# Sparse attention of a decoder trunk: branch order changed, compressed branch cut into 16 cells, window scores in row halves

## The reference, cut to what matters

```python
o_c = softmax(q @ ck.T * scale + bias, causal) @ cv      # 63 compressed keys per group
imp = sum over the group's heads of p_c @ ov             # importance of the 16 blocks of 64 keys
idx = top_k(forced or imp, 8)                            # 8 selected blocks per query
o_s = softmax over the keys of the selected blocks
o_w = softmax over the last 512 keys (sliding window)
o   = gate[0] * o_c + gate[1] * o_s + gate[2] * o_w
```

## Time and profile before

| | us |
|---|---|
| median of 3 runs | 2625.72 (2622.18 to 2634.36) |
| profiled execution | 2626.59 |
| its span | 2624.8 |

### The profile page before, as it was taken

How to read it: one execution, slowest core, us unless ns; L and a number is a source line. 1 busy time by engine, 2 the same in 40 slices (tenths; PEclk the granted TensorE clock), 3 DMA queues, 4 the chain that set the end, 5 groups by cost and what they waited for, 6 DMA issues and landing times. The chain is left out here.

```text
span 2624.8 us, 37850 instructions
## 1 busy us (share of the span) xinstructions
PE 2527.2 (96%) x14000; PEld 2049.3 (78%) x14000; DVE 1785.7 (68%) x2826; ACT 1124.4 (43%) x2184; POOL 1174.9 (45%) x889
## 2 busy tenths in 40 slices
PE   8999889999999999999988999999999999999999
PEld 5777667888887878887876688888788888777887
DVE  6554755477678999853059567666546767899993
ACT  4626544253334434323135566666524333433431
POOL 5362666234445444442236444444633444444441
PEclk8999999999999999999987899999999999999999
DMA  4010003224343544230342423222132334354531
GB/s 168 33 49 33 1 1 117 93 81 161 140 169 134 188 170 146 83 127 32 102 118 65 129 59 100 54 54 54 56 125 79 146 135 170 109 209 149 175 125 65
DMA packets 90973, 275.76 MB, mean 105 GB/s; under 512 B 9879, under 2 KB 38935, under 8 KB 76135
## 3 DMA queue, kind: packets, MB, share of 16 engines
q1 hardware_dynamic: 87240, 255.18, 28.4%
q10 hardware_dynamic: 3552, 18.18, 1.8%
HBM read 197.50 MB, written 73.86 MB: 103 GB/s over the span
## 5 line engine op out<-in xcount | busy, mean ns | idle before, releaser
L1582 PE MATMUL ps<-U_hi,RH 128*128 128x512 f32 x912 | 356.7, 391 | 12.5 <-DVE H L905 4.8
L1586 PE MATMUL ps<-U_lo,RH 128*128 128x512 f32 x912 | 355.7, 390 | 0.0
L1587 PE MATMUL ps<-U_hi,RL 128*128 128x512 f32 x912 | 355.6, 390 | 0.0
L1040 POOL TENSOR_TENSOR RL<-RAW,RH 128x512 fp32r<-128x512 f32 x112 | 156.2, 1395 | 395.2 <-ACT RH L744 395.2
L744 ACT ACTIVATE RH<-RAW 128x512 fp32r<-128x512 f32 x280 | 175.5, 628 | 292.8 <-PE ps L1587 285.4
L1533 POOL TENSOR_SCALAR PX<-PX,rinv,GATE 128x640 f32<-128x640 f32 (+7 forms) x256 | 197.8, 783 | 209.0 <-DVE rinv L3303 209.0
L1582 PE MATMUL ps<-U_hi,W_hi 128*128 128x512 f32 (+2 forms) x656 | 261.9, 399 | 13.3 <-DVE U_lo L2805 10.7
L1582 PE MATMUL ps<-SH,RH 128*128 128x512 f32 x656 | 256.8, 392 | 8.2 <-DVE H L905 4.1
L1586 PE MATMUL ps<-U_lo,W_hi 128*128 128x512 f32 (+2 forms) x656 | 258.2, 394 | 0.0
L1587 PE MATMUL ps<-U_hi,W_lo 128*128 128x512 f32 (+2 forms) x656 | 258.1, 393 | 0.0
L1586 PE MATMUL ps<-SL,RH 128*128 128x512 f32 x656 | 255.9, 390 | 0.0
(11 more groups left out here) (390 smaller groups left out, 6005.9 us busy)
## 6 DMA issues: line engine op xcount, KB each, us to landing
W_raw<-in_pieces SPq DMA_DIRECT2D x30, 1024.0 KB, 5.1
RAW<-in_pieces SPq DMA_DIRECT2D x28, 1024.0 KB, 4.9
RAW<-in_pieces SPq DMA_DIRECT2D x56, 512.0 KB, 7.7
hid_d<-HOA SPq DMA_DIRECT2D x24, 1024.0 KB, 3.9
hid_d<-HOB SPq DMA_DIRECT2D x24, 768.0 KB, 5.4
RHA<-hid_d SPq DMA_DIRECT2D x12, 1024.0 KB, 5.1
RHB<-hid_d SPq DMA_DIRECT2D x12, 768.0 KB, 6.6
U_rawh<-hid_d SPq DMA_DIRECT2D x12, 768.0 KB, 4.8
```

Source lines behind the costliest of these rows:

```text
L1040: G_.tensor_tensor(ring(RL[i], n), quarter(n, (B22, B11)[i - 5]), ring(RH[i], n).bitcast(F32), ALU.subtract).then_inc(u_lop.sem, 1)
L1582: m = mm(o, a_hi, b_hi, start=first, stop=False, skip_group_check=again)
L1586: mm(o, a_hi, b_lo, start=False, stop=False, skip_group_check=again)
L1587: return mm(o, a_lo, b_hi, start=False, stop=last, skip_group_check=again)
```

## The change

Names kept; `SEL` and `WIN` steps no longer alternate: steps 0 to 63 are the window steps of all eight pairs, 64 to 127 the selected ones. The compressed branch is cut into 16 cells, one per pair of heads and half of the queries; cell c has its scores at step 4 + 4c and its further parts `lag` steps later. Everything that PE turns through banks 4 and 5 (queries, keys, probabilities, cells, mask) stands in one list `SEQ`, and each waits until the one two before it is copied out.

```diff
-        STEPS = [x for k in range(NT) for x in ((SEL, NT - 1 - k), (WIN, NT - 1 - k))]
+            s = U // 2
+            br, i = (WIN if s < N_BR else SEL), NT - 1 - s % NT
+        def cell(s, lag):
+            c, r = divmod(s - 4 - lag, 4)
+            return c if r == 0 and 0 <= c < N_CELL else None
+        def query_of(s):
+            return [(p, h) for p in range(1, N_PAIR) for h in range(2) if s == 8 * p - 6 + h]
+        def imp_of(s, lag):
+            return [g for g in range(NG) if s == 32 * g + lag]
+        def rot(*x):
+            return 4 + NO[x] % 2
```

```diff
+                if br == WIN:
+                    for q, keys in ((pair_high(p), KW2), (pair_high(p), KWS), (pair_low(p), KW2)):
+                        for c0, c1 in parts:
+                            for e in range(2):
+                                rows = slice(DK * e, DK * e + DK)
+                                m = mm(bank(2 * e, 2)[:, c0:c1], q[rows, i * P:(i + 1) * P],
+                                       keys[rows, g, k0 * P + c0 - at_:k0 * P + c1 - at_], ...)
             for s in range(N_STEP + 1):
+                if s + 2 < N_STEP:
+                    scores(s + 2)
                 if s < N_STEP:
                     turn_p(2 * s)
+                for p, h in query_of(s):
+                    turn_q(p, h)
                 ...
                 if s:
                     weigh_p(s - 1)
                 if s < N_STEP:
                     turn_p(2 * s + 1)
+                if cell(s, 9) is not None:
+                    cmp_weigh(cell(s, 9))
+                ... imp_turn at lag 41, imp_sum at 42, imp_mask at 48 and 49
+                for e in range(2):
+                    if cell(s, 6 + e) is not None:
+                        cmp_turn(cell(s, 6 + e), e)
+                if cell(s, 0) is not None:
+                    cmp_scores(cell(s, 0))
```

The start on PE:

```diff
+            compress(0)
+            turn_q(0, 0)
+            turn_q(0, 1)
+            turn_k(0)
+            turn_k(1)
+            compress(1)
+            turn_gates()
+            turn_k(2)
+            turn_k(3)
+            compress_out()
+            scores(0)
+            turn_k(4)
+            turn_k(5)
+            scores(1)
+            turn_k(6)
+            turn_k(7)
```

DVE (bias, inverse and bias come first, as before) and ACT:

```diff
+                for p, h in query_of(s):
+                    q_low(p, h)
+                if cell(s, 1) is not None:
+                    cmp_max(cell(s, 1))
+                if cell(s, 3) is not None:
+                    cmp_sum(cell(s, 3))
+                if cell(s, 5) is not None:
+                    cmp_clamp(cell(s, 5))
+                ... choose(g, part) at lags 42 to 47
                 if s < N_STEP:
                     copy_p(2 * s + 1)
+                if cell(s, 9) is not None:
+                    cmp_out(cell(s, 9))
+                if cell(s, 0) is not None:
+                    cmp_bias(cell(s, 0))
+                if s % 4 == 0 and s > N_BR:
+                    put_out(s // 4 - 1 - N_CELL)
@@ ACT: copy_p(2s), q_high, expo(2s+4), expo(2s+5), then
+                if cell(s, 2) is not None:
+                    cmp_exp(cell(s, 2))
+                ... cmp_turned(cell(s, 6 + e), e), mask_turned
+                if s % 4 == 0 and 0 < s <= N_BR:
+                    window_out(s // 4 - 1)
```

```diff
+            for s in range(N_STEP):
+                normalise(2 * s)
+                normalise(2 * s + 1)
+                if cell(s, 1) is not None:
+                    below_max(cell(s, 1))
+                if cell(s, 4) is not None:
+                    share(cell(s, 4))
+                if cell(s, 5) is not None:
+                    add_up(cell(s, 5))
+                    gate_p(cell(s, 5))
+                if s < 4:
+                    stack_high(s)
+                if s % 8 == 6 and (s + 10) // 8 < N_PAIR:
+                    stage_q((s + 10) // 8)
+                ... s == 50 and s == 66: memset of QLM2 and of QLM, once read and saved
+                ... s == N_STEP - NT + 0, 2, 4, 6: split_high, split_low, split_high, split_low
```

```diff
+            sp.wait_ge(q_zero, 1)
+            load_q(2)
+            load_q(3)
+            sp.wait_ge(e_add, N_CELL)
+            load_bias(2)
+            load_bias(3)
+            for hd in (4, 5):
+                load_q(hd)
+                load_bias(hd)
             save_mask(1)
             for p in range(P_OUT1, P_OUT1 + 2):
                 load(0, p)
+            for hd in range(6, NH):
                 load_q(hd)
                 load_bias(hd)
```

More of the change, by code:

```diff
@@ L344, in build_program @@
         w_in, t4_in, ki_in = sem("cmp_w_in"), sem("cmp_T4_in"), sem("block_rows_in")
-        c_tp, c_mm, c_gelu, c_out, c_sm, c_sd, c_gate = (
-            sem("cmp_" + x) for x in "TP mm gelu out small sd gate".split())
+        c_tp, c_mm, c_gelu, c_sm, c_sd = (sem("cmp_" + x) for x in "TP mm gelu small sd".split())
         gd_in = sem("gains_in")
@@ L1514, in _ @@
-            pool.wait_ge(c_sm, 8)
-            for n in range(NH + 2):
-                if n % 2 == 0 and n // 2 + 2 < NH // 2:
-                    stage_q(n // 2 + 2)
-                if n >= 2:
-                    add_up(n - 2)
-                    gate_p(n - 2)
-                if n < NH and max_on_pool(n):
-                    below_max(n)
-            pool.wait_ge(e_qk, NH)
-            for k in range(2):
-                pool.wait_ge(t_sv[k], 32 * (NH // 2))
-            pool.wait_ge(e_gated, NH)
@@ new lines, in cmp_turn, with cmp_weigh @@
+            def cmp_turn(c, e):
+                b = room("t", c, e)
+                pe.wait_ge(e_gated, c + 1)
+                for t in range(4):
+                    m = nc.tensor.transpose(ps[0:NCMP, b, t * P:t * P + P], PC[c % 4][:, 3 - t, e, :], ident)
+                m.then_inc(turned, 1)
+            def cmp_weigh(c):
+                b = room("w", c)
+                pe.wait_ge(e_tpev, 2 * c + 2)
+                for e in range(2):
+                    m = mm(ps[DK * e:DK * (e + 1), b, :].rearrange("p (t n) -> p t n", t=4), CV[:, 2 * (c // 2) // HPG, :], PTC[e],
+                           start=True, stop=True)
+                m.then_inc(turned, 1)
@@ new lines, in imp_turn, with imp_sum @@
+            def imp_turn(g, h):
+                b = room("it", g, h)
+                pe.wait_ge(e_gated, 8 * (g + 1))
+                for t in range(4):
+                    m = nc.tensor.transpose(ps[0:NCMP, b, t * P:t * P + P], PACC[g][:, NT - 1 - (4 * h + t), :], ident)
+                m.then_inc(turned, 1)
+            def imp_sum(g):
+                b = room("is", g)
+                pe.wait_ge(i_tpev, 2 * g + 2)
+                for t in range(NT):
+                    m = mm(ps[:, b, t * NSEL:(t + 1) * NSEL], KVD[0:NCMP, t, 2, :], cs[0:NCMP, C_OV:C_OV + NSEL],
+                           start=True, stop=True)
+                m.then_inc(turned, 1)
```

1015 lines of the change are left out of this document (509 added, 506 removed).

## The result

The changed kernel takes 2701.66 us in the median of four runs (2693.41 to 2702.54), the kernel before 2627.43 in the four beside them (2622.18 to 2634.36). The ratio is 1.0261, 95% interval 1.0235 to 1.0287. The forecast was 2642, range 2592 to 2680: the direction is right, the size is 60 us short. The profiled execution took 2701.7, its span 2699.9.

What follows compares the result with a forecast made beforehand. TensorE (PE) was taken to bound the kernel, 2527 of 2624.8 us busy. The attention terms summed to 578 to 579 us against 563, +16, so the forecast was 2642 us, range 2592 to 2680.

Steps and rivals of the forecast that it cites:

- the new wait: Window steps: PE stands for POOL's late normalising, 39 us, and for room in banks 4 and 5, 5 us.
- POOL's chain: Window steps s = 1 mod 4: POOL's cell work delays normalising; fifteen stands of 2.6 us, 39 us, bounds 0 and 50.
- The clock: Start-up: a dip of the clock that lasts into the first steps, 8 us, bounds 0 and 20.
- Rival C: The clock stays low longer: another dip like that of 44 us costs up to 22, giving 2664 us; chance 0.10.
- PE's own time: Window phase: PE's work 237 us, less 2.6 for scores done in start-up, plus 10 for small bubbles.
- row halves: Window scores as three passes of parallel half-array matmuls: 14.5 us won, 15 lost by changes of array shape.
- start-up: From the last input projection to the first transpose of probabilities: 37 us.
- selected pairs: Selected phase: each pair of heads takes 27.7 us, eight pairs 221 us.
- wait for the q rows of heads 6 and 7: Selected phase, near s = 86: SP loads these heads behind mask 1 and output weights; PE waits 8 us.
- level with PE: Window phase: DVE needs 28 us per pair of heads beside PE's 29 to 30, so its waits are paid.
- A: Rival: POOL and DVE run far enough ahead, the 39 + 5 us stay away, giving 2598 us; chance 0.24.
- B: Rival: row halves are not parallel; all serial 2685 us, only loads serial 2659 us; chance 0.12.

Runs made afterwards that it cites:

- e6_rooms_back: c2_lags with the cell items put back directly behind the turned probabilities, ACT's and DVE's order to match: median 2648.30 us.
- e5_chain_back: c2_lags with clamp, below_max, add_up and gate_p (DVE and POOL) put back at the changed kernel's steps: median 2667.80 us.
- c2_lags: Changed kernel with below_max later, clamp earlier, cell items behind PV, heads 6 and 7 loaded earlier, last weight splitting later: median 2623.78 us.

## Why the prediction was right in direction and wrong in size

**The step that failed** is the last sentence on the new wait: "The two banks 4 and 5 now rotate over cells too ... 5 us in all." I priced one delay, an exp on ACT ahead of the emptying of a cell, and not the plain rule that the change had written into `SEQ`: an item placed directly behind a `turn_p` that has just filled both banks stands until the first is copied, 0.4 to 1.6 us each time. The runs show 39 us of waits for room in the window stretch, and e6_rooms_back shows 27 us of time for the cell items alone.

**POOL's chain** was right in mechanism and path, hand-over by hand-over: 8.3 to 8.7 us from the step's start, and 8.4 measured (1536.95 to 1545.36). Booked 39 us; its waits are 20.4 in the window stretch, and with the start's 3.2 the 23.6 of the row, since PE was already late by the banks. Taken by itself (e5_chain_back) it costs 41.8 of time, 26.6 of that in waits. That 39 and 41.8 lie close is luck: the forecast counted waits alone.

**The clock** was the second mis-sized term: 8 us booked, for one dip. The window stretch of the changed kernel has 49.6 us at half clock, in nine dips; at 0.46 that is some 23 us (an estimate from the slope above). In c2_lags it is 5.1. Rival C (one long dip, against PE busy 39 of 44 us) did not come; many short ones did, such as the one behind the stand of 1543.7 to 1545.4. Before, 82 us of half clock stood in this region, so the change gave back some and lost it again.
The Trainium skill, "TensorE: Matmul & The Clock Gate", section "A second HAM failure mode: psum-queue depth-cycling", describes a kernel whose cycling through PSUM banks idles PE so often for moments that the clock swings between its levels. The runs here agree in part: with the cell items' waits for banks put back alone (e6_rooms_back) half clock is 27.9 us of the attention stretch, without them 7.5 (c2_lags). But POOL's stands alone do it too, with 42.4 (e5_chain_back).

**PE's own time** was low by some 16 us: busy 283.0 less 23 for the clock is 260 against 244 (-2.6 + 237 + 10). The row halves make up about half: forecast -14.5 + 15 = 0, measured 6 to 8 us lost. The couples are as parallel as assumed. But the entry into half-array shape costs 0.18 us (0.26 against 0.08), the way out 0.09 (the last pass of 256 columns takes 0.21 to the first transpose, where 0.12 is usual) and the slower transposes 0.07: 0.33 us a step of five blocks, some 21 in all (an estimate, 64 times that), where I had taken 0.24 from the column halves. The other half I did not place.

In sum for the window stretch: banks 39 instead of 5 (+34), POOL and the first stand 24 instead of 39 (-15), clock 23 instead of 8 (+15), own time +16: +50 of the 51. The own time is what is left of the busy time, so that the terms meet the total shows nothing by itself.

**Right:** start-up (35.6 against 37), selected pairs at 27.9 to 28.1 against 27.7, one wait for the q rows of heads 6 and 7 (6.6 against 8, though with the dip that came with it it cost nearer 10), outputs and window biases at nothing. In the two first selected pairs cell 15, the importance and mask of group 1 cost some 14 us and not 6.5; the end cost 4 (the wait of 3.7 for POOL) and not 8. DVE "level with PE" was wrong: busy 197.5 of 347.0, 24.7 us a pair of heads and not 28, and in c2_lags 198.0 of 289.9. What ends PE's waits is DVE's and POOL's order, not their load.

**Rivals.** A was the right question: with chain and bank waits away it would be 2598, and the kernel without most of them (c2_lags) takes 2624. Its window stretch is 37 us above A's (289.9 against 296.4 - 44): 14 by what PE still stands (24.3 us against 10 for small bubbles), the rest by its own time; from the first selected PV on it is 13 below (231.2 against 244.5). B is refuted: couples mostly 3 or 4 ns apart.

## What to carry to other kernels

Where several users rotate through few buffers, write down for each place in the list how long after the filling of the buffer two before it comes: put a long operation that uses no such buffer (here PV) between them, and one user in each gap. Only steps that filled both buffers at once made others stand. Before cross-engine work is slipped into a loop, trace the one queue in which it stands ahead of the loop's own work; a missing step of lag made PE stand at every fourth step. When several stalls lie in one loop, removing one shows only part of its worth: look which other wait has grown (here a load far behind), and judge each by putting it back into the clean version.

## What the runs showed of the hardware

A stand of PE can be paid twice. During the 6.6-us wait the granted clock fell to half, and 4.6 us of work ran at it; with only POOL's stands put back into the clean order (e5_chain_back), half clock rose from 7.5 to 42.4 us. One us at half clock goes with 0.41 to 0.46 us in a dense stretch, read from twelve profiles of the same matmuls. Half-array work by rows starts in couples mostly 3 or 4 ns apart, but at these sizes (256 and 384 columns, three passes against two) the entry, exit and slower transposes around it (0.33 us in a step of five blocks) eat the whole gain.
